# First modulation by channel blocks: a unit of weights, two transposed blocks, their chunks, then the next unit

## What is computed

```python
mod = silu(c) @ w_mod[l] + b_mod[l]          # c_ctx for the context tokens
shift, scale, gate = split(mod, 3)
h = x * (1 + scale) + shift
proj = h @ w_in[l]                           # its first 1536 columns go to the long convolution
filt = hyena_filters(...)                    # two small sine layers, a product with w3, times a decay
y_hy = hyena(hy_in, conv_w, conv_b, filt, skip)   # short convolution, then products of spectra
```

## Time and profile before

| what | us |
|---|---|
| median of 3 runs | 1950.26 |
| lowest, highest | 1948.79, 1950.71 |
| the profiled execution | 1950.17 |
| its span | 1948.4 |
| TensorE busy in the span | 1817.4 |
| VectorE busy | 1133.0 |
| ScalarE busy | 664.3 |
| moved by DMA | 150.00 MB |

### The profile page before, as it was taken

The page is one execution under the profiler, slowest core; times in us unless marked ns, Lnnn a source line. Parts: engine busy times, 40 slices in busy tenths (PEclk is TensorE's granted clock), DMA queues, the critical chain, the costliest instruction groups (busy, mean ns, idle before and its releaser), DMA issues.

```text
span 1948.4 us, 27784 instructions
## 1 busy us (share of the span) xinstructions
PE 1817.4 (93%) x11336; PEld 1580.1 (81%) x11336; DVE 1133.0 (58%) x1582; ACT 664.3 (34%) x1148; POOL 456.7 (23%) x210
## 2 busy tenths in 40 slices
PE   5999999999999999999969999999999999999995
PEld 3787899886877777999856969997878677789995
DVE  5599893545243444486877989825434444435834
ACT  3424312444224444212243342234433344442121
POOL 0100032212230111467211001322223211115650
PEclk8999999999999999999979999999999999999998
DMA  8110021211310111354520102211122011115331
GB/s 342 44 54 33 33 98 60 65 38 45 114 44 20 33 33 39 123 191 142 208 87 33 55 33 76 77 60 50 44 79 79 22 36 33 34 44 187 128 109 54
DMA packets 48493, 150.00 MB, mean 77 GB/s; under 512 B 9386, under 2 KB 10922, under 8 KB 47600
## 3 DMA queue, kind: packets, MB, share of 16 engines
q1 hardware_dynamic: 44768, 134.09, 19.7%
q10 hardware_dynamic: 3600, 14.16, 2.1%
HBM read 141.63 MB, written 6.59 MB: 76 GB/s over the span
## 4 chain that ended last, share of the span: by engine, by line
PE 69%; DVE 22%; ACT 4%; issue 4%; DMA 1%; POOL 1%; SPq 0%; ACTq 0%; DVEq 0%; POOLq 0%
PE PS L798 16%; PE PS L803 15%; PE PS L799 15%; PE PS L852 4%; PE PS L841 3%; PE PS L1101 2%; PE PS L886 2%; PE PS L883 2%; PE PS L1034 2%; PE PS L865 2%; DVE Wl L1467 1%; DVE st L1446 1%; DVE MG L1697 1%; DMA pmod_w<-in_w_mod 1%; PE PS L1090 1%
## 5 line engine op out<-in xcount | busy, mean ns | idle before, releaser
L1857 POOL TENSOR_TENSOR Wl<-W,Wh 128x1024 fp32r<-128x1024 f32 (+1 forms) x166 | 375.1, 2261 | 1343.3 <-ACT Wh L1152 1263.0
L798 PE MATMUL PS<-Hh,Wh 128*128 128x320 f32 x2048 | 612.7, 314 | 16.8 <-ACT Wh L1152 8.9
L799 PE MATMUL PS<-Hl,Wh 128*128 128x320 f32 x2048 | 604.4, 310 | 0.0
L798 PEld LDWEIGHTS PS<-Hh,Wh 128*128 128x128 f32 x2048 | 386.2, 189 | 41.1 <-issue 26.4
L799 PEld LDWEIGHTS PS<-Hl,Wh 128*128 128x128 f32 x2048 | 386.6, 189 | 0.6 <-issue 0.5
L803 PE MATMUL PS<-Hh,Wl 128*128 128x320 f32 x2048 | 321.4, 310 | 0.9 <-POOL Wl L1857 0.9
L803 PEld LDWEIGHTS PS<-Hh,Wl 128*128 128x128 f32 x2048 | 305.5, 188 | 1.4 <-POOL Wl L1857 1.4
L1446 DVE TENSOR_REDUCE st<-PS 128x1 f32<-128x640 f32 (+1 forms) x160 | 114.9, 718 | 318.6 <-PE PS L865 176.0
L1152 ACT ACTIVATE work<-PS 128x640 f32<-128x640 f32 (+9 forms) x298 | 172.5, 592 | 257.7 <-PE PS L803 68.3
L1152 ACT ACTIVATE Wh<-W 128x1024 fp32r<-128x1024 f32 x196 | 184.9, 948 | 60.1 <-PE PS L803 26.8
L1289 ACT ACTIVATE th<-PS 128x640 f32<-128x640 f32 x64 | 45.1, 705 | 367.3 <-PE PS L803 367.3
(11 more groups left out here) (211 smaller groups left out, 2487.4 us busy)
## 6 DMA issues: line engine op xcount, KB each, us to landing
W<-in_w_in SPq DMA_DIRECT2D x132, 512.0 KB, 3.5
W<-in_w_branch SPq DMA_DIRECT2D x48, 256.0 KB, 2.6
work<-in_w_mod_rows ACTq DMA_DIRECT2D x23, 512.0 KB, 3.7
pmod_w<-in_w_mod SPq DMA_DIRECT2D x8, 1024.0 KB, 12.9
W<-in_w_out SPq DMA_DIRECT2D x16, 512.0 KB, 4.1
late_modulation_w<-in_w_mod_rows SPq DMA_DIRECT2D x9, 512.0 KB, 5.7
work<-in_x_sample SPq DMA_DIRECT2D x2, 2048.0 KB
x_mid<-work SPq DMA_DIRECT2D x1, 2560.0 KB, 8.5
```

Of the source, the lines that this page charges most:

```text
L798: pe.matmul(out, Wh[:, b, kk, :], xh[:, kk, t], start=kk == 0, stop=False)
L799: pe.matmul(out, Wh[:, b, kk, :], xl[:, kk, t], start=False, stop=False)
L1857: return pool.tensor_tensor(out, in_, high.bitcast(f32), ALU.subtract)
```

## The change

The first modulation is cut by channels instead of by kind. The tiles of `w_mod` are laid out so that one pmrow gives scale and shift of two blocks: unit u is pmod u, ht 2u, ht 2u+1, two 2u, pmrow u+1, two 2u+1. `ffn` 1 stands behind two 0, filt 0 behind two 5, filt 1 between two 6 and two 7; filt 2 to 4 and the fdfts take layer 1's order. VectorE's wait for scale and shift asks for four columns a unit. `pmod_w` has four buffers in other places (two in `MG`, two in `work`), `cpad` lies in `work`. The load order becomes pmod_w 0 and 1, weight tiles 0 and 1, X, pmod_w 2 to 5, w3 and the decays, pmod_w 6 and 7, then, behind a wait for pmrow 2, the DFT tables. ScalarE does the decays' exponentials in `filt` 0 instead of `lam`. VectorE makes both low parts of the first two weight tiles ahead of ht 0's wait, and in layer 0 the two low parts of a unit's blocks in its odd ht.

```diff
 def layer_steps(l):
     if l == 0:
-        p = [("pmod", g) for g in range(4)]
-        f = [("ffn", 0), ("ffn", 1)] + [("filt", t) for t in range(NT)] + [("fdft", i) for i in range(5)]
-        rows = [("pmrow", g) for g in range(4)]
-        s = [("lam", 0)] + f[:1] + rows[:1] + f[1:2] + rows[1:2] + p[:1] + rows[2:3] + p[1:2] + f[2:4] + rows[3:] + p[2:3]
-        s += f[4:5] + p[3:] + start_steps([], {2: f[5:6], 4: f[6:7]})
-        s += [("conv", 0), ("conv", 1), ("fdft", 0), ("fdft", 1), ("conv", 2), ("fdft", 2), ("conv", 3), ("fdft", 3), ("fdft", 4)]
+        f = [("filt", t) for t in range(NT)]
+        s = [("lam", 0), ("ffn", 0)]
+        for u in range(4):
+            a, b = 2 * u, 2 * u + 1
+            s += [("pmrow", 0)] * (u == 0) + [("pmod", u), ("ht", a), ("ht", b), ("two", a)]
+            s += [("ffn", 1)] * (u == 0) + ([("pmrow", u + 1)] if u < 3 else f[1:2]) + [("two", b)] + (f[0:1] if u == 2 else [])
+        s += f[2:3] + [("conv", 0), ("conv", 1)] + f[3:4] + [("conv", 2)] + f[4:] + [("conv", 3)]
+        s += [("fdft", i) for i in range(5)]
...
-NP = 5
+NP = 4
...
+        cpad = area(work, 20000, KD, 32)
+        pmod_w = [area(MG, 2048 * n, 2, KD, 128) for n in range(2)] + [area(work, 13328 + 2048 * n, 2, KD, 128) for n in range(2)]
...
             layer_tables(0, 0)
             for g in range(2):
                 first_modulation(g)
-            layer_tables(0, 1)
-            for g in range(2, NP):
-                first_modulation(g)
-            load_x(0)
-            for g in range(NP, KD):
-                first_modulation(g)
             weight(0)
             weight(1)
+            load_x(0)
+            for g in range(2, 6):
+                first_modulation(g)
+            layer_tables(0, 1)
+            for g in range(6, KD):
+                first_modulation(g)
+            sp.wait_ge(*filled(0, "pmrow", 2))
             layer_tables(0, 2)
...
+            def first_decay(l):
+
+                act.wait_ge(filter_here, 16 * N_FILTER * (l + 1))
+                link(act.activation(expld, expld, ACT.Exp))
+                act.activation(decay, expld[:, :, 0, :], ACT.Exp, scale=negt[:, 0:1]).then_inc(sems["decay_ready"], 1)
...
-                        act.wait_ge(filter_here, 16 * N_FILTER * (l + 1))
-                        link(act.activation(expld, expld, ACT.Exp))
-                        act.activation(decay, expld[:, :, 0, :], ACT.Exp, scale=negt[:, 0:1]).then_inc(sems["decay_ready"], 1)
+                        if l:
+                            first_decay(l)
...
+                        if i == 0 and l == 0:
+                            first_decay(l)
...
-                            m = 4 * i + j
+                            m = 2 * i + j // 2 + KD * (j % 2)
...
-                        if i == 0:
+                        if l == 0 and i == 0:
+                            low_part(l, 0)
+                            low_part(l, 1)
+                        if l == 0 and i % 2 == 0:
+                            dve.wait_ge(*after("ss_ready", l, 2 * i + 4))
+                        elif i == 0:
                             dve.wait_ge(*after("ss_ready", l, 2 * KD))
...
-                        if l == 0 and i < 2:
-                            low_part(l, i)
-                        for c in [i - 1] * (i > 0) + [i] * (i == KD - 1):
+                        for c in [i - 1] * (i > 0) + [i] * (i == KD - 1) if l else (i - 1, i) if i % 2 else ():
```

More of the change, by code:

```diff
@@ L430, in build @@
         Hl = sb("Hl", [128, KD, NTOK], f32r)
-        pmod_w = sb("pmod_w", [128, NP, 2, KD, 128], over=Hh_at)
         late_w = sb("late_modulation_w", [128, 5, D], over=Hh_at + 4 * 5120)
@@ L436, in build @@
         Wl = sb("Wl", [128, 2, KD, 128], f32r)
-        cpad = sb("cpad", [128, KD, 32], over=Wl_at)
         MG = sb("MG", [128, KD * NTOK])
@@ L661, in first_modulation @@
                     sp.wait_ge(*filled(0, "pmrow", (g - NP) // 2))
-                sp.dma_start(pmod_w[:, g % NP], A["w_mod"][0, 2 * g:2 * g + 2].rearrange("m p k n -> p m k n"))\
+                sp.dma_start(pmod_w[g % NP], A["w_mod"][0, 2 * g:2 * g + 2].rearrange("m p k n -> p m k n"))\
                   .then_inc(pmod_here[g % NP], 16)
@@ L900, in _ @@
                                 last = pe.matmul(ps[32 * j:32 * j + 32, 0:128], cpad[:, k, :],
-                                                 pmod_w[:, (2 * i + j // 2) % NP, j % 2, k, :], start=k == 0, stop=k == KD - 1)
+                                                 pmod_w[(2 * i + j // 2) % NP][:, j % 2, k, :], start=k == 0, stop=k == KD - 1)
                         last.then_inc(full_of(l, kind, i), 1)
@@ L1478, in _ @@
             dve.wait_ge(c_sig, 1)
-            link(dve.memset(cpad[:], 0.0))
+            link(dve.memset(cpad, 0.0))
             TT(cpad[:, :, 0:2], ccol[:], csig, ALU.mult).then_inc(c_silu, 1)
@@ L1949, in laid_out @@
         "w3": x["hy_ffn_w3"].reshape(DEPTH, HY_FFN, 2, 2 * HY).transpose(0, 2, 1, 3).reshape(DEPTH, 128, 2 * HY),
-        "w_mod": tiles(x["w_mod"][0:1, :, 0:2 * D]),
+        "w_mod": tiles(x["w_mod"][0:1, :, 0:2 * D]).reshape(1, 2, KD, 128, KD, 128).transpose(0, 2, 1, 3, 4, 5).reshape(1, 2 * KD, 128, KD, 128),
         "w_mod_rows": np.concatenate([x["w_mod"][0, :, 2 * D:], x["w_mod"][1, :, 0:2 * D], x["w_mod"][1, :, 2 * D:]], -1)
```

## The result

| | before | after |
|---|---|---|
| median, us | 1949.53 (4 runs, 1945.91 to 1950.71) | 1964.45 (4 runs, 1959.74 to 1966.50) |
| ratio of the two, 95% interval | | 1.0076 [1.0054, 1.0099] |
| span of the profiled execution | 1948.4 | 1962.9 |
| conv 0's copy starts | 71.95 | 76.46 |
| last spectrum copy starts | 111.10 | 122.48 |

The change makes the kernel 14.9 us slower. The forecast of +8.3 had the sign right and was too small, and 1964.45 lies above the range of 1951.7 to 1963.5.

A forecast was written before the change was run, and what follows sets the result against it. TensorE, busy 1817 of 1948 us, was taken as the bound, with a chain across engines up to 111.10. Conv 0's copy 4.15 us later plus 4.1 behind it gave +8.3, so 1958.5 us; range 1951.7 to 1963.5.

The forecast's parts named there:

- Transfers, unit 0: Start of layer 0: X in at 20.4 us, chunk 0 at 24.5, no transfer on the path from X on.
- Units 1 and 2: First modulation: pmod 1 waits for VectorE's ffn argument; chunk 2 at 40.05 us, chunk 4 at 51.7, both at the low clock.
- The filter ahead of ht 6: Unit 3: decays and filt 0 stand before pmod 3 and ht 6; chunk 6 at 68.8 us, conv 0's copy at 76.1.
- What follows, +4.1: Conv 0's copy to last spectrum copy: 43.27 us, priced from layer 1's rows, against 39.15 before, as three taps are owed.
- The part on the unknown clock: Low level taken at chunks 2, 4, 6; high through units 1 and 2 gives -4.4 us, low all along +5.5.
- The order behind that point is untouched, so the change is worth what it does to the moment of that row.: Behind the last spectrum copy (111.10 us before): the same row distances as before, so nothing added there.
- Low clock throughout: Rival: groups of 3.5 to 7 us with waits keep the clock low; +13.8 us, 1964; chance 0.08 for +12 to +15.
- The rule of the Trainium skill: Modulation chunks: short groups of matmuls parted by waits each start at the low clock; time at the sum or above.
- The sum: Whole kernel: 4.15 up to conv 0's copy plus 4.1 behind it, +8.3 us on 1950.17, so 1958.5.
- the chain's 4.15: Layer 0 up to conv 0's copy: it starts at 76.1 us instead of 71.95, 4.15 later.

## Why the prediction was wrong, point by point

- *Transfers, unit 0.* Right: X's transposes 20.78 (20.4), chunk 0 25.07 (24.5), none of pmrows 1 to 3 waits for a transfer.
- *Units 1 and 2.* Right within 0.8 us: the Sin ahead of the row copy and TensorE's wait for it (36.06, predicted 35.55), chunk 2 at 39.98 (40.05), pmrow 2 at 43.48 (43.4), chunk 4 at 52.33 (51.7), both at the low clock, pmrow 3 at 55.72 with 1.96 us (55.0, 2.2). The one surprise, pmrow 1 at the full clock (1.96), hides in the same wait.
- *The filter ahead of ht 6.* Right, and the largest delay on the chain up to conv 0: decay made by 62.4 (62.0), VectorE free 65.2 (64.7), chunk 6 at 69.17 (68.8), conv 0's copy at 76.46 (76.1), behind the decay that it was to wait for. Chunk 6 started 5.9 us earlier with the taps and decays off this place, and the loss was gone with them.
- *What follows, +4.1.* The step that failed. The mechanism (three taps are still owed) and the price with a steady clock were right, as two kernels with this order gave 43.24 and 43.28. But the term measured 6.9 here. "Word for word that of layer 1, so its rows give the price" took equal order for equal waits. In layer 1 TensorE waits 1.36 us once, after long unbroken work, and its clock stays at 1.00. Here the decay for filt 2 holds conv 0's copy back, as the prediction itself had worked out one paragraph earlier (76.1 instead of 74.5), so TensorE waits 1.45 and 1.36 us, and the clock fell to 0.50. With both waits filled the stretch took 43.48. The part on the unknown clock bounded chunks, rows and "the end" and left this tail out, although its waits are of the kind that was bounded elsewhere.
- *"The order behind that point is untouched, so the change is worth what it does to the moment of that row."* The second failure, +3.1 in the traces. The row distances behind it did not stay: the clock falls at later joints, and they fall differently in each execution, by up to 4.4 us for the same kernel. One profiled execution was taken as the kernel's whole. Whether the changed kernel has a longer rest of its own is open: both its traces have 1840.4 and 1840.0, but the fourteen traces lie between 1832.9 and 1842.9 in no order of delay, and one of two plain delays added nothing.
- *The rivals.* Low clock throughout (1964) came nearest in time by luck, for another reason: the clock was low at chunks 2 and 4 as forecast, not throughout, and pmrows 1 and 3 ran at the full level. The rule of the Trainium skill named there ("TensorE: Matmul & The Clock Gate", section "HAM oscillation — how this bites in real kernels") put the time at the sum or above it; by that rule, the trace agrees, in the chunks and even more in the taps behind them (2.10 us against 1.25). With a tap laid into the gaps chunks 2 and 6 started at the full clock and the time was that of the kernel before, while the groups stayed.
- *The sum.* 4.5 + 6.9 + 3.1 = 14.5 instead of 4.15 + 4.1 = 8.3: 0.35 from the chain, 2.75 from the clock in the tail, 3.1 from behind. The 0.35 is less than what conv 0's copy moves by between traces; against the second trace of the changed kernel (75.37) the chain's 4.15 was 0.7 too high.

## What to carry to other kernels

When a step order is split into groups, look first at what small step on another engine now stands ahead of the next group's input; here two exponentials, once hidden under the loads, and four vector operations stood ahead of chunk 6, which started 5.9 us earlier without them. A price taken from a twin stretch holds only with the twin's waits and at the twin's clock: list the waits of both, and give each wait of a copied stretch the same bounds as the waits of the new one. And a stretch that isn't changed is not a constant when its joints are near a fall of the clock: its spread between executions of one kernel belongs in the range.

## What was not expected of the hardware

The same joint, with equal work and waits to 0.01 us, was followed by the full clock in one execution and by the low one in the next (granted 1.00 and 0.66 over 510 to 520 us). Two waits, of 1.45 and 1.36 us, with a tap of 1.25 us between them were enough for a fall in four of four traces, while one wait of 1.36 us, or one of 0.68 and one of 1.36 us, behind longer unbroken work held 1.00. Twenty extra matmuls, 3.4 us of work on the bounding engine, made the stretch 2.5 us shorter.
